# First attention's causal mask: from a matmul into bias tables of eight key blocks

## What the kernel computes

```python
def fox_branch(qb, kb, vb, log_f):
    c = jnp.cumsum(log_f, axis=1)
    ...
        causal = key_pos[None, :] <= q_pos[:, None]
        logits = jnp.einsum('bqhd,bshd->bhqs', q_blk, kb).astype(jnp.float32) * scale
        logits = logits + jnp.transpose(cq_blk, (0, 2, 1))[..., None] - c_k[:, :, None, :]
        logits = jnp.where(causal[None, None], logits, NEG)
        probs = jax.nn.softmax(logits, axis=-1).astype(vb.dtype)
```

## Time and profile before

| | us |
|---|---|
| median of three runs | 1215.03 |
| the profiled execution | 1216.24 |
| its span | 1214.4 |
| TensorE busy | 1194.1 (98%) |
| VectorE busy | 617.4 (51%) |
| ScalarE busy | 550.3 (45%) |
| GpSimd busy | 511.0 (42%) |
| TensorE's 32 mask matmuls, first and last start | 129.4 and 179.0 |

### The profile page before, as it was taken

One profiled execution on the slowest core, in us unless ns is written; L12 is line 12 of the kernel. 1 busy time (PEld: TensorE's weight loads), 2 busy tenths in 40 slices (PEclk: granted clock), 3 DMA queues, 4 the chain that ended last, 5 costly groups with the idle time before them and its releaser, 6 DMA issues.

```text
span 1214.4 us, 15669 instructions
## 1 busy us (share of the span) xinstructions
PE 1194.1 (98%) x5840; PEld 992.8 (82%) x5840; DVE 617.4 (51%) x1459; ACT 550.3 (45%) x989; POOL 511.0 (42%) x280
## 2 busy tenths in 40 slices
PE   9999999999999999999999999999999999999998
PEld 8878778888888887689878788788888888888886
DVE  5789874774528264984973774845222231220002
ACT  6553574476523364445774785434322232231113
POOL 1428462344443424134252873443444434443441
PEclk9999999999999999999999999999999999999999
DMA  8204662202332523143122304233332332323221
GB/s 267 82 31 140 174 174 70 104 1 72 120 104 70 198 79 104 35 142 124 36 40 71 103 2 155 90 102 103 97 100 81 105 105 90 103 86 121 95 78 70
DMA packets 80475, 119.19 MB, mean 98 GB/s; under 512 B 16008, under 2 KB 42760, under 8 KB 80016
## 3 DMA queue, kind: packets, MB, share of 16 engines
q1 hardware_dynamic: 80400, 118.19, 30.4%
HBM read 107.67 MB, written 4.21 MB: 92 GB/s over the span
## 4 chain that ended last, share of the span: by engine, by line
PE 85%; DVE 7%; ACT 3%; POOL 3%; issue 2%; DMA 1%; SPq 1%; DVEq 0%; ACTq 0%; POOLq 0%
PE bank L1720 64%; PE bank L2041 9%; PE bank L1784 2%; PE bank L1816 2%; PE bank L1862 2%; PE bank L1798 2%; DVE sc L1421 2%; DVE m L1417 1%; PE bank L1760 1%; POOL w_lo L703 1%; POOL w_lo L686 1%; PE bank L1901 1%; ACT w_hi L806 0%; DVE mqT L1595 0%; PE bank L1754 0%
## 5 line engine op out<-in xcount | busy, mean ns | idle before, releaser
L686 POOL TENSOR_TENSOR w_lo<-w_raw,w_hi 128x2048 fp32r<-128x2048 f32 (+4 forms) x81 | 362.7, 4478 | 579.2 <-ACT w_hi L774 521.8
L1720 PE MATMUL bank<-aH,w_hi 128*128 128x512 f32 x800 | 318.3, 398 | 1.9 <-DVE mqT L1595 1.1
L1720 PE MATMUL bank<-aH,w_lo 128*128 128x512 f32 x800 | 311.9, 390 | 0.0
L1720 PE MATMUL bank<-aL,w_hi 128*128 128x512 f32 x800 | 308.7, 390 | 0.0
L774 ACT ACTIVATE w_hi<-w_raw 128x2048 fp32r<-128x2048 f32 (+4 forms) x77 | 142.6, 1852 | 263.8 <-PE bank L1720 162.2
L1720 PEld LDWEIGHTS bank<-aL,w_hi 128*128 128x128 f32 x800 | 150.2, 188 | 32.1
L1720 PEld LDWEIGHTS bank<-aH,w_hi 128*128 128x128 f32 x800 | 150.7, 188 | 31.1 <-issue 3.2
L1720 PEld LDWEIGHTS bank<-aH,w_lo 128*128 128x128 f32 x800 | 150.6, 188 | 26.6 <-issue 0.2
L1170 DVE TENSOR_TENSOR fg<-bank,rB 128x512 f32<-128x512 f32 x22 | 15.1, 691 | 128.2 <-PE bank L1720 128.2
L1720 PE MATMUL bank<-w_hi,aH 128*128 128x512 f32 (+4 forms) x224 | 77.3, 345 | 0.3 <-POOL w_lo L686 0.3
L1720 PE MATMUL bank<-uH,w_hi 128*128 128x512 f32 x192 | 75.0, 391 | 0.5 <-DVE uL L1616 0.5
(11 more groups left out here) (338 smaller groups left out, 2122.5 us busy)
## 6 DMA issues: line engine op xcount, KB each, us to landing
w_raw<-in_w_in SPq DMA_DIRECT2D x23, 1024.0 KB, 5.0
w_raw<-in_w_gate SPq DMA_DIRECT2D x22, 512.0 KB, 3.8
w_raw<-in_w_up SPq DMA_DIRECT2D x22, 512.0 KB, 4.7
w_raw<-in_w_down SPq DMA_DIRECT2D x11, 1024.0 KB, 4.8
w_raw<-in_w_merge SPq DMA_DIRECT2D x8, 1024.0 KB, 4.9
w_raw<-in_w_out SPq DMA_DIRECT2D x8, 1024.0 KB, 5.0
w_raw<-in_w_ple_gate SPq DMA_DIRECT2D x4, 1024.0 KB, 4.9
w_raw<-in_w_in SPq DMA_DIRECT2D x4, 512.0 KB, 7.9
```

Of the source, the lines that this page charges most:

```text
L686: pool.tensor_tensor(out=w_lo[:, c % 2, 0:n], in0=w_raw[:, c % 2, 0:n], in1=w_hi[:, c % 2, 0:n].bitcast(F32), op=ALU.subtract).then_inc(w_ ...
L1720: ins = pe.matmul(o, l, r, start=(kk == 0 and operand == ROUNDED and m == 0), stop=(kk == total - 1 and operand == REST), skip_group_check ...
```

## The change

Each head's bias becomes a table of eight key blocks of 128 columns. SyncE loads blocks 2 to 5 (the row's four blocks) and block 0 (its first again) with two DMAs. VectorE writes the masked blocks with three additions of the 128x128 diagonal mask: blocks 1 and 6 from 3 and 4 in one instruction of 256 columns, block 5 in place, and block 7 from 2. Unit b then reads its b+1 blocks with a start and a step: block 7; blocks 0, 1; blocks 0, 3, 6; blocks 2 to 5. The additions for head 0 stand before the attention, those for head h+1 in the fourth unit of head h, behind the wait for that unit's scores and ahead of its reduction. The matmul of the mask, the two casts and the wait for them go. The two tables lie at 98 and 127 (in KB a partition); the space of the bf16 tables is kept as a pad.

```diff
     return next(i for i in range(NU + 9) if side_count(name, i) >= step)
+MASKED_FROM = ((1, 7, 5, 3, 5, 1), (5, 6, 1, 5, 6, 1), (7, 8, 1, 2, 3, 1))
+BIAS_OF = ((7, 8, 1), (0, 2, 1), (0, 7, 3), (2, 6, 1))
+
+
 PAIR_HI_AT, PAIR_LO_AT = {6: 2, 14: 3}, {6: 2, 14: 3}
...
         pT = place("pT", 44, [P, 2, PT_W, P], F32R)
-        cB = place("cB", 98, [P, 2, S])
+        cB = [place(f"cB{i}", at, [P, 2 * NB, P]) for i, at in enumerate((98, 127))]
         tmA = place("tmA", 0, [P, NB, S])
...
         gains_landed, cst_landed, small_landed, p_landed = sem("gains_landed"), sem("cst_landed"), sem("small_landed"), sem("p_landed")
-        ones_ready, half_ready = sem("ones_ready"), sem("half_ready")
+        ones_ready, bias_masked = sem("ones_ready"), sem("bias_masked")
         sq_ready, sum_ready, rt_ready = sem("sq_ready"), sem("sum_ready"), sem("rt_ready")
...
             def load_cum(h):
-                sp_.dma_start(cB[:, h % 2, :], cum_dram[h:h + 1, :].broadcast_to([P, S])).then_inc(cum_landed[h % 2], 16)
+                for first, n in ((2, NB), (0, 1)):
+                    row = cum_dram[h:h + 1, 0:n * P].broadcast_to([P, n * P])
+                    dst = cB[h % 2][:, first:first + n, :].rearrange("p c k -> p (c k)")
+                    sp_.dma_start(dst, row).then_inc(cum_landed[h % 2], 16)
             def stack_head(h):
...
                         wait_filled(dve, name + ".l", i)
+                        shaped = [t[:, 0:n] if name != "fox" else t[:, 0:n].rearrange("p (c k) -> p c k", k=P)
+                                  for t in (sc_[:, i % RING, :], bank_of(name + ".l", i))]
                         empties(dve.tensor_tensor_reduce(
-                            out=sc_[:, i % RING, 0:n], in0=bank_of(name + ".l", i)[:, 0:n], in1=k_bias(h, b),
+                            out=shaped[0], in0=shaped[1], in1=k_bias(h, b),
                             scale=1.0, scalar=-3e38, op0=ALU.add, op1=ALU.max, accum_out=mx[:, i:i + 1]),
...
             rms(1)
-            dve.tensor_copy(ident16[:], ident[:])
-            dve.tensor_copy(diag16[:], tab("causal")[:, 3 * P:4 * P]).then_inc(half_ready, 1)
             dve.wait_ge(small_landed, 32)
...
                                                  op0=ALU.mult, op1=ALU.subtract), "vb", b)
+            def mask_bias(h):
+
+                dve.wait_ge(cum_landed[h % 2], 32 * (h // 2 + 1))
+                for o0, o1, o_step, i0, i1, i_step in MASKED_FROM:
+                    t, given = cB[h % 2][:, o0:o1:o_step, :], cB[h % 2][:, i0:i1:i_step, :]
+                    n = i1 - i0
+                    mask = tab("causal")[:, 3 * P:4 * P].rearrange("p (o k) -> p o k", o=1).broadcast_to([P, n, P])
+                    dve.tensor_tensor(out=t, in0=given, in1=mask, op=ALU.add).then_inc(bias_masked, 1)
+
             def fox_bias(h, b):
                 if b == 0:
-                    dve.wait_ge(cum_landed[h % 2], 16 * (h // 2 + 1))
-                return cB[:, h % 2, 0:(b + 1) * P]
+                    dve.wait_ge(bias_masked, 3 * h + 3)
+                if b == 3 and h + 1 < H:
+                    mask_bias(h + 1)
+                first, end, step = BIAS_OF[b]
+                return cB[h % 2][:, first:end:step, :]
             for q in range(2):
                 low_half(UNITS["ga"][0] + 1, q)
+            mask_bias(0)
             softmax("fox", sp, pT, fox_bias, low_rows, attB)
...
                             ins = pe.matmul(o, q, k, start=(m == 0), stop=(m == len(pairs) - 1))
-                        if name == "fox":
-                            ins = pe.matmul(o[:, b * P:(b + 1) * P], ident16[:], diag16[:], start=False, stop=True,
-                                            skip_group_check=True)
                         fills(ins, name + ".l", i)
...
             pe.wait_ge(cst_landed, 32)
-            pe.wait_ge(half_ready, 1)
             pe.wait_ge(split_lo, NB)
```

More of the change, by code:

```diff
@@ L21 @@
 F32R = mybir.dt.float32r
-BF16 = mybir.dt.bfloat16
 ALU = mybir.AluOpType
@@ L315, in build @@
         ident = sb("ident", [P, P])
-        ident16 = sb("ident16", [P, P], BF16)
-        diag16 = sb("diag16", [P, P], BF16)
+        sb("pad0", [P, P])
         ones = sb("ones", [P, P])
```

## The result

| | before | changed |
|---|---|---|
| median of the runs, us | 1214.99 (1213.47 to 1215.74, 6 runs) | 1222.39 (1220.14 to 1223.6, 6 runs) |
| ratio, 95% interval | | 1.0060 (1.0049 to 1.0072) |
| profiled execution: time, span, clock | 1216.24, 1214.4, 0.998 | 1221.94, 1220.2, 0.996 |

The account below looks back on a forecast made before the run. TensorE was taken to lead except in two stretches set by VectorE and SyncE; there reduction delay 1.0, issue 0.42 and hold 1.25, less 0.1, gave +2.5 to 2.6 us: 1217.6, range 1214.0 to 1218.8.

Parts of the forecast that it names:

- the work that goes: Over the first attention: 32 short mask matmuls leave TensorE, 0.46 us a head, 3.7 us in all, a gain only where TensorE leads.
- the casts: Two bf16 casts go from 31 us; VectorE's operation at 33.21 escapes GpSimd's subtraction, freeing over 4 us, worth nothing.
- the additions and the reduction: Per head: three additions delay the fourth unit's reduction by 0.73 us; the stepped operand costs it nothing; unit 3's ends +0.9.
- the hold: Unit 23: the third addition waits until GpSimd's weight subtraction ends, 1.25 us more, bounded between 0 and 1.3.
- rival A: Unit 23: the third addition gets in ahead of GpSimd, no hold; +1.3 us, 1216.3; chance 0.28.
- The rule that was weighed: Unit 11: by the shared-port lock, additions also wait 0.38 us for GpSimd's scalings; sum would be 1217.7.
- the issue: SyncE: one more table load costs 0.42 us of issue ahead of six head loads, bounds 0 and 1.56.
- the landing itself is covered: Table loads: masked a head (6.4 to 6.9 us) after issue, landing in 3.3 to 4.7, so landing adds nothing.
- what ends the stage: Before head 7: unit 23's reduction 1.0 later, issue 0.42, hold 1.25; the chunk of qa lands about 2.65 us late.
- B: Head 4's loads: a long SyncE issue moves head 4 some 1.1 us; with the hold +3.4, 1218.4; chance 0.14.
- C: Additions cost nothing, running while VectorE would have waited; about -1.2 us, 1213.8; chance 0.11.
- D: TensorE's work alone counts, head loads and chunk coming before it asks; 3.7 us faster, 1211.3; chance 0.07.

## Why the prediction was wrong, step by step

**Right: the work that goes.** 0.46 us a head, by the kernel without the mask matmuls.

**Right in value, wrong in working: the casts.** The VectorE operation was to start ahead of GpSimd's subtraction and escape. It didn't. The pair came at 32.62 and 32.56, still 0.06 apart, and took 4.81 us again. Timelines of GpSimd and VectorE in the changed kernel:

```profile
32.56 4.59 POOL L691 TENSOR_TENSOR w_lo<-w_raw,w_hi 128x2048 fp32r<-128x2048 f32 x1 [6.44 <-ACT w_hi L779]
```

```profile
32.62 4.81 DVE L1212 TENSOR_TENSOR tmI<-tmI,rp 128x256 f32<-128x256 f32 x1
```

VectorE isn't early at all: the casts' time lay in a wait for ScalarE further on (0.37 us at 30.82). Neither mattered.

**Right: the additions and the reduction.** Three take 0.75 to 0.83 recorded (0.34 + 2 x 0.2 is 0.74, not 0.73; nothing hangs on it). The stepped operand costs nothing, as taken. The reduction of unit 3 ends 1.0 later once the early start is taken out, against 0.9.

**Right: the hold.** In unit 23, of the changed kernel, VectorE and GpSimd:

```profile
167.79 1.90 DVE L1455 TENSOR_TENSOR cB<-cB,cst 128x256 f32<-128x256 f32 x3
```

```profile
168.27 1.28 POOL L708 TENSOR_TENSOR w_lo<-w_raw,w_hi 128x512 fp32r<-128x512 f32 x1 [0.97 <-ACT w_hi L811]
```

1.1 us over the usual 0.83, against 1.25, so rival A is out. The additions alone cost 2.5 us; the forecast's two terms for them at the end of the stage, 0.73 and 1.25, make 2.0. The changed kernel has a hold that was not forecast, 1.47 us in unit 27 (175.26), but there TensorE waits for head 7's loads anyway.

**The rule that was weighed.** By the Trainium skill ("SBUF — State Buffer", section "SBUF: two separate sides") GpSimd's row scalings would hold additions too. The changed kernel doesn't show it, since its sets overlap no scaling by more than 0.1 us unless a subtraction runs first. The kernel with additions alone does, in unit 11 as the forecast had it. Timelines of VectorE and GpSimd:

```profile
143.83 0.99 DVE L1450 TENSOR_TENSOR cX<-cB,cst 128x256 f32<-128x256 f32 x3
```

```profile
143.18 1.30 POOL L718 TENSOR_SCALAR sp<-sp,rsum 128x512 f32<-128x512 f32 x2
```

Both are longer than usual, the three additions by 0.16 us (0.83) and the two scalings by 0.25 (1.05 in the earlier trace rows). In the kernel with the additions behind the reduction a scaling of 256 columns that starts 0.06 behind an addition takes 0.82 instead of 0.48, and the three additions take 1.02. So the traces agree that scalings and additions hold each other. The price for VectorE was less than the 0.38 that the forecast worked out with GpSimd never held.

**Right: the issue.** From SyncE's first issue to its last before head 2 it is 4.00 instead of 3.51 (133.14 to 137.14, for the last of before): 0.49 against 0.42.

**Wrong: "the landing itself is covered".** That sentence looked at who reads the table. It left out who stands behind it in the queue. The 6.83 us from reduction to landed loads were made of 6.40 + 0.42, with the last landing left at 2.80. It landed in 3.37 in the changed kernel, and this makes the 2.1 of head 2 whole (1.0 + 0.5 + 0.6). The two kernels with an added load tell its cause, the small table's short rows ahead of it. The forecast had 0 for this term, and no bound.

**Wrong: a wait costs only its length.** "A wait of over 1.5 us of TensorE for the head loads before head 2" was named as what would show the forecast right, and head 2 was priced as 1.3 us late. It was 2.99, and TensorE then ran from 142 to 144 us at half clock. Head 3 came 3.2 late, where it was to come 1.1 late (146.5 against 145.43). The clock stood nowhere in the sum.

**Wrong: what ends the stage.** The forecast kept the chunk of qa as the last link, 2.65 late. In the changed kernel ScalarE gets the chunk 6.05 late, and head 7's loads come later still. Three delays meet on one queue there: the unit 23 reduction, itself later because heads 2 to 6 are 3.7 late, the hold, and a last landing of 4.55 against a median of 3.4. The scores of unit 31 come at 185.21, where the earlier trace rows has 178.40: 7.4 us with the start taken out, the whole loss.

**Rivals.** B had the right direction (a later load for head 4) by another mechanism; no issue took 1.56 in the changed kernel's stage. Its long issue did come again elsewhere: 1.47 us among head 4's loads in the kernel with additions alone and 1.67 in the one with one load, and TensorE waited 0.17 and 1.09 us before head 4 there. C and D are out by the changed kernel's time, and D also by the kernel without mask matmuls: with no additions and no second load, 3.7 us of TensorE's work were worth 1.0 in the medians.

**What stays open.** Why head 7's last load took 4.55 us was not isolated; the kernel with a second load, which has the same packets, waited 0.72 us at head 7. The 2 us between the parts' sum and the change were not divided by a run; the estimate above gives 1.35 us to head 7's loads and the clock behind them. Whether the number of packets, their length or their partitions delay what stands behind them is open too. And the length of a wait alone doesn't tell whether the clock falls: the list below has both outcomes between 1.87 and 2.41 us.

## What to carry to other kernels

A small transfer put ahead of others in a queue can cost three times: its issue, its packets in front of what lands behind it, and whatever that wait sets off. So price it by the consumer of the *next* transfers, and prefer few long rows, or no transfer at all (with an on-chip copy in its place 3.9 us came back here). When TensorE's own work shrinks while its loads come later, the saved time turns into one long wait in place of steady work, and the wait of 2.99 us cost 1.3 us more in the clock behind it. Work that an engine gets in addition belongs behind the instruction that a queue waits for, not ahead of it (with one load, 3.3 us between the two places); but it then delays what that engine does next, and here that took the rest of the gain.

## What the runs showed of the hardware that was not expected

- With 144 more packets per table, 64 KB, ahead of six loads, the landing of those of fK went from 2.8 to 3.4 us (median). With the same 64 KB in 48 more packets it stayed at 2.8.
- The granted clock went to the 1.2 GHz level behind TensorE's waits of 2.99, 2.84, 2.46, 2.41, 2.05, 1.99 and 1.87 us in these kernels, and stayed at 2.4 GHz behind others of 2.38, 2.19, 1.94 and 1.89.
- A plain fp32 matmul of 512 columns took 0.87 us, in two records; the projection's fp32r ones start 0.23 apart.
- GpSimd's row scaling and VectorE's additions of two SBUF operands lengthened each other: 0.82 instead of 0.48 us for a scaling of 256 columns, 1.02 instead of 0.82 for three additions.
- VectorE's copy of 128 columns took 0.22 us alone and 0.99 beside GpSimd's subtraction (172.49 to 173.76), so the hold is not only for operations with two inputs from SBUF. Timeline of VectorE, kernel with one load:

```profile
165.46 0.22 DVE L1451 COPY cB<-cB 128x128 f32<-128x128 f32 x1
...
172.86 0.99 DVE L1451 COPY cB<-cB 128x128 f32<-128x128 f32 x1
```
